# A feature pass by seven products per quadrant scheme, in two halves of tokens

## The reference, cut to what matters

```python
xn = _rms_norm(x, norm_g[l]) * (1.0 + sc_x) + sh_x
fx_in, fx_gate, qx, kx, vx, nx_gate = _split_proj(xn @ w_in[l])   # 1024 -> 6 x 512
qx = _rms_norm(_heads(qx), q_norm_g[l])                             # heads of 64
kx = _rms_norm(_heads(kx), k_norm_g[l])
f_out = _fourier(fx_in, w_four[l]) * jax.nn.silu(fx_gate)
na_out = _neighbourhood_attention(qx, kx, vx, ...) * jax.nn.silu(nx_gate)
```

## Time and profile before

| | us |
|---|---|
| median of three runs | 3400.0 (3398.42 to 3401.95) |
| profiled execution, device time | 3402.36 |
| its span, first to last instruction | 3400.6 |
| TensorE busy in it | 3111.9 (92%) |
| VectorE busy in it | 1514.0 (45%) |
| ScalarE busy | 941.8 (28%) |
| GpSimd busy | 795.5 (23%) |

### The profile page before, as it was taken

How to read it: one execution, slowest core, us unless ns; L and a number is a source line. 1 busy time by engine, 2 the same in 40 slices (tenths; PEclk the granted TensorE clock), 3 DMA queues, 4 the chain that set the end, 5 groups by cost and what they waited for, 6 DMA issues and landing times. The chain is left out here.

```text
span 3400.6 us, 39668 instructions
## 1 busy us (share of the span) xinstructions
PE 3111.9 (92%) x14503; PEld 2445.2 (72%) x14503; DVE 1514.0 (45%) x2504; ACT 941.8 (28%) x1520; POOL 795.5 (23%) x842
## 2 busy tenths in 40 slices
PE   3799999999988999775998999899999898999899
PEld 2588887888876666553897877677888675666687
DVE  6643333042306666386455222476000145777633
ACT  4422212110112334342222234322011133555400
POOL 5322222111112222265342222011111041000111
PEclk7899999999998999778898999999999998999999
DMA  7534335122243341314102666323211235776475
GB/s 272 184 97 116 102 101 180 61 77 75 75 127 87 90 105 55 90 47 97 43 26 82 200 185 208 109 112 123 74 74 74 99 102 134 155 158 142 112 199 148
DMA packets 325559, 390.82 MB, mean 115 GB/s; under 512 B 93879, under 2 KB 260264, under 8 KB 310696
## 3 DMA queue, kind: packets, MB, share of 16 engines
q1 hardware_dynamic: 320692, 387.11, 39.9%
q10 hardware_dynamic: 4704, 1.59, 0.2%
HBM read 256.77 MB, written 135.79 MB: 115 GB/s over the span
## 5 line engine op out<-in xcount | busy, mean ns | idle before, releaser
L691 PE MATMUL f_psum_out<-f_x_high,f_w_high 128*128 128x512 f32 (+1 forms) x1472 | 573.5, 390 | 18.8 <-DVE f_x_low L668 8.1
L691 PE MATMUL f_psum_out<-f_x_low,f_w_high 128*128 128x512 f32 (+1 forms) x1472 | 569.0, 387 | 0.0
L691 PE MATMUL f_psum_out<-f_x_high,f_w_low 128*128 128x512 f32 (+1 forms) x1472 | 568.6, 386 | 0.0
L691 PEld LDWEIGHTS f_psum_out<-f_x_high,f_w_high 128*128 128x128 f32 x1472 | 279.1, 190 | 77.9 <-issue 15.0
L691 PEld LDWEIGHTS f_psum_out<-f_x_low,f_w_high 128*128 128x128 f32 x1472 | 278.9, 189 | 56.5 <-issue 1.7
L691 PEld LDWEIGHTS f_psum_out<-f_x_high,f_w_low 128*128 128x128 f32 x1472 | 278.9, 189 | 55.5
L1351 PE MATMUL nbr_psum_o<-nbr_probT,nbr_v 128*128 128x512 f32 (+3 forms) x576 | 235.8, 490 | 0.0
L683 POOL CAST f_w_high<-f_w 128x1024 fp32r<-128x1024 f32 x41 | 42.6, 1040 | 747.8 <-PE f_psum_out L691 550.5
L532 PE MATMUL p_psum_proj<-p_w_high,p_h_high 128*128 128x512 f32 x512 | 207.5, 405 | 7.4 <-issue 4.0
L532 PE MATMUL p_psum_proj<-p_w_low,p_h_high 128*128 128x512 f32 x512 | 202.1, 395 | 0.0
L532 PE MATMUL p_psum_proj<-p_w_high,p_h_low 128*128 128x512 f32 x512 | 202.1, 395 | 0.0
(11 more groups left out here) (541 smaller groups left out, 6134.0 us busy)
## 6 DMA issues: line engine op xcount, KB each, us to landing
f_w<-in_w_fm SPq DMA_DIRECT2D x45, 512.0 KB, 5.7
side_ada_w<-in_w_ada_rows SPq DMA_DIRECT2D x24, 512.0 KB, 5.7
scratch_qkmT<-p_qkT_out SPq DMA_DIRECT2D x32, 384.0 KB, 4.6
scratch_z1T<-f_out SPq DMA_DIRECT2D x10, 1024.0 KB, 4.8
p_z<-scratch_z1T SPq DMA_DIRECT2D x16, 640.0 KB, 6.6
p_xt<-in_x SPq DMA_DIRECT2D x16, 512.0 KB, 3.9
p_staging<-in_w_tok SPq DMA_DIRECT2D x8, 1024.0 KB, 8.0
scratch_hT<-p_h_slot SPq DMA_DIRECT2D x16, 512.0 KB, 3.3
```

The source lines that it names most:

```text
L691: last = nc.tensor.matmul(self.p_out[b][:, n * BANK + lo:n * BANK + hi], self.w_parts[b][w_part][:, k, :], self.x_parts[x_part][:, n, k, l ...
```

## The change

The feature pass is made of 24 items: two halves of 1024 tokens by twelve pairs of blocks, in the order of `F2_ORDER`, so in each half first four pairs of queries and keys, then v, Fourier input and gates. An item's two blocks, the halves of its 1024 inputs, and pairs of neighbouring token tiles make two by two quadrants. The Strassen-Winograd scheme computes the four quadrants of the result from seven products of quadrants or of sums of quadrants. Each product is 4 x 3 matmuls of 128x512 into one of four PSUM banks (`product`); VectorE merges the banks into output rows in SBUF (`merge`: a copy for the first, one addition for each of the others and two for the sixth). The sums of weight quadrants are made by GpSimd for each item (`add_weights`), the seven high parts by ScalarE, the low parts by GpSimd. The sums of input quadrants (t1 to t4) are made once for each pair of tiles in the token pass by GpSimd (`combine`; the last pair by VectorE) and stored beside three quadrants as they are, so that seven arrays of 1 MB a half are loaded. The second half's arrays replace the first's during item 11.

An item's sums of squares have two matmuls for each row and lie at the start of the next item (row 1) and behind its first product (row 0). VectorE takes the reciprocals in pieces of 512 columns between the merges of the next item. Before the barrier four products of item 0 are done.

```diff
@@ -717,6 +717,117 @@
...
+class QuadrantPass:
+    A11, A12, A22, S1, S2, S3, S4 = range(7)
+    B11, B21, B22, T1, T2, T3, T4 = range(7)
+    PRODUCTS = ((A11, B11), (S2, T2), (A12, B21), (S3, T3), (A22, T4), (S1, T1), (S4, B22))
+    N, HK, BANKS = 7, KB // 2, 4
...
+    def load_x(self, sp, half, i):
+        if half:
+            sp.wait_ge(self.prod_ready, self.N * (half * self.per_half - 1) + i + 1)
+        sp.dma_start(self.x[i][0][:].rearrange("p t k c -> p (t k c)"),
+                     self.x_dram[self.PRODUCTS[i][1], :, half * 4 * BANK:(half + 1) * 4 * BANK]).then_inc(self.x_in[i], 16)
+
+    def round_x(self, act, half, i):
+        act.wait_ge(self.x_in[i], 16 * (half + 1))
+        self.nc.scalar.activation(self.x[i][1][:], self.x[i][0][:], ACT.Copy).then_inc(self.x_rounded, 1)
+
+    def rest_of_x(self, dve, half, i):
+        dve.wait_ge(self.x_rounded, self.N * half + i + 1)
+        self.nc.vector.tensor_tensor(self.x[i][2][:], self.x[i][0][:], self.x[i][1][:], ALU.subtract).then_inc(self.x_ready, 1)
...
+    def add_weights(self, pool, n):
+        nc, w = self.nc, self.w[n % 2]
+        a11, a12, a21, a22 = (w[:, m, k:k + self.HK] for m in range(2) for k in (0, self.HK))
+        s1, s2, s3, s4 = (self.sums[:, i] for i in range(4))
+        pool.wait_ge(self.w_in[n % 2], 16 * (n // 2 + 1))
+        pool.drain()
+        nc.gpsimd.tensor_tensor(s1, a21, a22, ALU.add)
+        nc.gpsimd.tensor_tensor(s3, a11, a21, ALU.subtract)
+        pool.drain()
+        nc.gpsimd.tensor_tensor(s2, s1, a11, ALU.subtract)
+        pool.drain()
+        nc.gpsimd.tensor_tensor(s4, a12, s2, ALU.subtract).then_inc(self.sums_ready, 1)
+
+    def round_w(self, act, n, i):
+        a = self.PRODUCTS[i][0]
+        if n:
+            act.wait_ge(self.prod_ready, self.N * (n - 1) + i + 1)
+        if a < self.S1:
+            act.wait_ge(self.w_in[n % 2], 16 * (n // 2 + 1))
+        else:
+            act.wait_ge(self.sums_ready, n + 1)
+        self.nc.scalar.activation(self.a_high[:, i], self.quadrant(n, a), ACT.Copy).then_inc(self.a_rounded, 1)
+
+    def rest_of_w(self, pool, n, i):
+        pool.wait_ge(self.a_rounded, self.N * n + i + 1)
+        self.nc.gpsimd.tensor_tensor(self.a_low[:, i], self.quadrant(n, self.PRODUCTS[i][0]), self.a_high[:, i], ALU.subtract)\
+            .then_inc(self.a_ready, 1)
+
...
+    def product(self, pe, n, i):
+        pe.wait_ge(self.a_ready, self.N * n + i + 1)
+        if n % self.per_half == 0:
+            pe.wait_ge(self.x_ready, self.N * (n // self.per_half) + i + 1)
+        if self.N * n + i >= self.BANKS:
+            pe.wait_ge(self.prod_free, self.N * n + i + 1 - self.BANKS)
+        a_parts, x_parts = (self.a_high, self.a_low), self.x[i][1:]
+        for k in range(self.HK):
+            for at, (w_part, x_part) in enumerate(PASSES):
+                last = self.nc.tensor.matmul(self.bank(n, i), a_parts[w_part][:, i, k, :], x_parts[x_part][:, :, k, :],
+                                             start=(k == 0 and at == 0), stop=(k == self.HK - 1 and at == len(PASSES) - 1))
+        last.then_inc(self.prod_ready, 1)
...
@@ tile_pass_2
+    def combine(eng, ops, j):
+
+        b11, b21, b12, b22 = (slot[b][:, k:k + HK] for b in range(2) for k in (0, HK))
+        t1, t2, t3, t4 = (combined[:, n] for n in range(4))
+        eng.wait_ge(combined_stored, 16 * (j + 1))
+        ops.tensor_tensor(t1, b12, b11, ALU.subtract)
+        ops.tensor_tensor(t3, b22, b12, ALU.subtract)
+        eng.drain()
+        ops.tensor_tensor(t2, b22, t1, ALU.subtract)
+        eng.drain()
+        ops.tensor_tensor(t4, t2, b21, ALU.subtract)
+        eng.drain().then_inc(combined_ready, 1)
...
+                else:
+                    sp.dma_start(quadrants[:, 2, of_pair], slot[1][:, HK:].rearrange("p k c -> p (k c)")).then_inc(slot_stored[1], 16)
+                    wait_apart(sp, combined_ready, j + 1, taken)
+                    sp.dma_start(quadrants[:, 3:7, of_pair], combined[:].rearrange("p s k c -> p s (k c)")).then_inc(combined_stored, 16)
...
+            def begin_next():
+                sp.wait_ge(w_ready, MB)
                 for b in range(2):
+                    sp.wait_ge(slot_stored[b], 16 * (NT // 4 + 1))
+                sp.wait_ge(combined_stored, 16 * (NT // 4 + 1))
+                fp.load_w(sp, 0)
+                fp.load_x(sp, 0, 0)
+
+            def go_on():
+                sp.wait_ge(gated[1], PAIRS)
+                fp.load_w(sp, 1)
+                sp.wait_ge(mix_ready[1], PAIRS)
+                sp.wait_ge(o_ready, NT - 1)
+                fp.load_x(sp, 0, 1)
                 sp.wait_ge(slices_used, 1)
+                fp.load_x(sp, 0, 2)
+                fp.load_x(sp, 0, 3)
 
             for k in range(BUFFERS, MB):
                 sp.wait_ge(w_ready, k - BUFFERS + 1)
                 begun.load_w(sp, k)
+            tiles(sp, tile, begin_next, go_on)
+            sp.wait_ge(slices_used, 2)
+            fp.load_x(sp, 0, 4)
+            fp.load_x(sp, 0, 5)
+            fp.load_x(sp, 0, 6)
...
+            for i in range(fp.BANKS):
+                fp.product(pe, 0, i)
+                if i == 0:
+                    turn_x(NT - 1)
...
+                fp.round_x(act, 0, 0)
+                for i in range(fp.N):
+                    fp.round_w(act, 0, i)
+                    if i == 1:
+                        fp.round_x(act, 0, 1)
+                fp.round_x(act, 0, 2)
+                fp.round_x(act, 0, 3)
...
+                if b == 0 and not first:
+                    wait_apart(pool, x_filled, 2 * j, taken)
+                    combine(pool, nc.gpsimd, j - 1)
...
@@ feature_pass_2
+F2_ORDER = (0, 1, 2, 3, 4, 5, 6, 7, 8, 9, 10, 11)
...
+            for n in range(LAST + 1):
+                aside(n - 1, 1)
+                for i in range(N):
+                    if n or i >= fp.BANKS:
+                        fp.product(pe, n, i)
+                    if i == 0:
+                        aside(n - 1, 0)
...
+            def after(n, b):
+                if kind(n) == "qk":
+                    act.wait_ge(out_ready[b], n + 1)
+                    if among(n, "qk"):
+                        act.wait_ge(low_ready[b], among(n, "qk"))
+                    nc.scalar.activation(work[b][:], out[n % 2][b][:], ACT.Square).then_inc(sq_ready[b], 1)
...
+            def empty(n, b):
+                if kind(n) == "qk":
+                    act.wait_ge(sum_ready[b], among(n, "qk") + 1)
+                    nc.scalar.activation(work[b][:], p_aux[b][:], ACT.Sqrt, scale=1.0 / HD, bias=g.eps[:]).then_inc(rms_ready[b], 1)
+                    act.drain().then_inc(aux_free[b], 1)
...
+            for n in range(LAST + 1):
+                empty(n - 1, 1)
+                for i in range(N):
+                    if n < LAST:
+                        fp.round_w(act, n + 1, i)
+                    if i == 0:
+                        empty(n - 1, 0)
+                    if n == fp.per_half - 1 and i:
+                        fp.round_x(act, 1, i - 1)
+                    if i == 5:
+                        after(n, 1)
+                if n == fp.per_half - 1:
+                    fp.round_x(act, 1, N - 1)
+                after(n, 0)
...
+                elif i == 5:
+                    dve.drain()
+                    nc.vector.tensor_tensor(column(second, 1), whole(u3), bank(n, 5), ALU.add)
+                    nc.vector.tensor_tensor(whole(u2), whole(u2), bank(n, 5), ALU.add).then_inc(fp.prod_free, 1)
+                    dve.drain().then_inc(out_ready[1], 1)
+                elif i == 6:
+                    nc.vector.tensor_tensor(column(first, 1), whole(u2), bank(n, 6), ALU.add).then_inc(fp.prod_free, 1)
+                    dve.drain().then_inc(out_ready[0], 1)
...
+            for n in range(LAST + 1):
+                refill = n == fp.per_half - 1
+                invert(n - 1, 1, 0)
+                for i in range(3):
+                    merge(n, i)
+                invert(n - 1, 1, BANK)
+                norm(n - 1, 1)
+                for i in range(3, N):
+                    merge(n, i)
+                    if i == 3:
+                        invert(n - 1, 0, 0)
+                    if i == 4:
+                        invert(n - 1, 0, BANK)
+                    if i == 5:
+                        norm(n - 1, 0)
+                    if refill:
+                        fp.rest_of_x(dve, 1, i - 3)
+                if refill:
+                    for i in range(N - 3, N):
+                        fp.rest_of_x(dve, 1, i)
...
```

More of the change, by code:

```diff
@@ L2364, in _ @@
+            sp.wait_ge(high_stored, 32 * among(LAST + 1, "qk"))
+            for n in range(2):
+                for b in range(2):
+                    sp.wait_ge(stored[n][b], 16 * (LAST + 1) // 2)
         @block.tensor
         def _(pe):
[L2366 to L2373 removed]
@@ L2375, in turn_v @@
-            def turn_v(j, b):
-                pe.wait_ge(vT_ready[b], j - FIRST_V + 1)
-                for n in range(NT):
```

(6 more changed lines are left out.)

371 lines of the change are left out of this document (213 added, 158 removed).

## The result

The changed kernel took 3478.7 us (3475.1 to 3484.1, four runs) where the kernel before took 3401.0 in the same job: a ratio of 1.023 (95% interval 1.0212 to 1.0248, written in square brackets below), slower by 78 us. The forecast was 3455, in a range from 3385 to 3485: the time lies in it, 6 us under its upper end.

A forecast was written before the change was run, and what follows sets the result against it. The feature pass was taken as bound by its count of products. Terms -54.4 + 3.3 + 69 + 39 - 6 + 5 - 0.5 = +55 on a median of 3400.0 gave 3455 us, range 3385 to 3485.

The forecast's parts named there:

- Products: Feature pass: 2016 full products instead of 2304, 240 fewer behind the barrier at 0.2267 us each, -54.4 us.
- the rival of slow products: Feature pass: moving operand in four runs of 128 columns slows products 5%, 23 us more, 3478 us; chance 0.05.
- Rounds: Eight queries' and keys' items: VectorE sets the pace, 32 us a round against TensorE's 22.9, +69 us (+33 to +89).
- the rivals in which it doesn't: Queries' and keys' items: VectorE's round stays under TensorE's, so the saved products come through, 3386 us; chance 0.13.
- in which only its 26.6 us of work count: Queries' and keys' items: VectorE's pieces overlap without stalls, 3419 us; chance 0.15.
- sum without a slow start, 30.8: Queries' and keys' round: VectorE's work 26.6 us plus stalls of 2.4 and 1.8 us.
- The two stalls: Queries' and keys' round: VectorE idles 2.4 us for ScalarE's square root and 1.8 us for TensorE's third product.
- busy shares: Queries' and keys' items: VectorE busy over 80% and TensorE under 80%, as a sign of the forecast.
- Slow start of TensorE: Queries' and keys' rounds: low clock after idling delays the third product 1.7 us each round; without it 13 us lower.
- Token pass: SyncE waits for GpSimd's sums before the next loads, delaying y, 6.5 us six times, +39 us (+30 to +50).
- Handover: Last tile to work behind the barrier: about L + 49 instead of L + 54.8, -6 us (-12 to +3).
- refill: Between the halves: 7 MB of new input and VectorE's rests delay the first merge of item 12, +5 us (+2 to +12).

The follow-up runs named there:

- the halved reciprocals: Changed kernel with the second 512 columns of each row's reciprocal replaced by a multiply and add to a constant: 3443.4 us.
- The late store: Changed kernel with the store of the four input sums, and its wait for GpSimd, moved behind the next tile's loads in SyncE's queue: 3428.1 us.
- GpSimd small: Changed kernel with GpSimd's sums and low parts of the weights cut to 8 of each 128 columns from item 1 on: 3466.5 us.
- the first reordering: Changed kernel with mixed item order, row 1 normalised one item later, the late store, and pieces and weights rounded behind the last tile's work at handover: 3399.8 us.
- the third order: Changed kernel, VectorE reordered, with the late store; at handover pieces 1, 2 rounded before the last fill, weights, piece 3 behind: 3407.3 us; with the last order 3361.8.
- the last order: Changed kernel with mixed item order and normalising spread, row 1's reciprocals early behind the item's last merge: 3415.0 us; with the late store and the third order, 3361.8.

## Why the prediction was right

**Products.** Right: 19.0 us for each item of 84 products, so the rival of slow products is out. Its 3478 lies close to the result, but by chance of the sum.

**Rounds**, +69 forecast, +83.0 measured: six rounds of 33.0 to 34.4 us where 32 was taken, two of 31.4 where it was 30. The mechanism is the one named. That VectorE sets the pace in the tail is shown by the halved reciprocals (-45.3 us); the rivals in which it doesn't, or in which only its 26.6 us of work count, are out. The prediction's own sum without a slow start, 30.8, is what the two rounds without one show: 32.0, less 1.3 for GpSimd.

That 1.3 is the term that the prediction lacked. The trace before had none of GpSimd's work at that place, and I took VectorE's durations as they stood; beside GpSimd the subtraction of row 1 takes 2.14 us and its scaling 1.78. Taking GpSimd's work out shortened the tails by 10.2 us in sum, most of the 14 that were missing. The Trainium skill's "SBUF — State Buffer", section "Who interferes with whom", says that a VectorE instruction with two inputs in SBUF contends with a GpSimd instruction that reads SBUF; the trace agrees: the sixth merge (L2675), with one input in PSUM, takes 686 to 689 ns in all 24. That rule stood open to the prediction.

The two stalls were counted as VectorE's own, 2.4 us behind ScalarE and 1.8 behind TensorE, and added. In the round the first lies ahead of the second: without it, VectorE waits as much longer for TensorE. Undoing it gave nothing. The sum was right all the same, since only the moment at which the third product is ready counts: 13.6 us after the end of the sixth merge by the prediction, 14.9 from its start, and 15.1 measured. Its busy shares missed: VectorE over 80% and TensorE under 80% were forecast, and they are 75 and 79% against 80 and 76%.

**Slow start of TensorE.** It was counted at 1.7 us a round by the clock of the earlier trace rows, of which the taken 32 keeps 1.2. The rule of "TensorE: Matmul & The Clock Gate" in the Trainium skill, section "HAM oscillation", that it is paid in each round, agrees with the trace: behind each of the six waits of 8.67 us the sums took 3.48 to 3.75 us instead of 1.88. It is not paid in the first round of each half, which follows no such wait. In the six it costs 1.0 to 2.4 us, 1.85 in the mean, because the sums and the first three products lie in the head, where VectorE waits for TensorE. That is 11.1 us in sum and close to the 13 of the prediction. This is worked out from the rounds with and without it; keeping TensorE busy removed it in two rounds alone, and no run removed it in all.

**Token pass**, +39 forecast, +43.5 measured, by the mechanism named: SyncE waited 5.7 us for GpSimd's sums ahead of y. The late store takes it all back. In the turn shown y is issued 6.4 us behind the store of x2T instead of 0.73, so 5.7 later (5.1 forecast), and it lands 5.85 us after that instead of 4.39: over the six turns it lands 1.4 us later in the mean, with the bytes ahead of it (1 forecast). The two were not tried apart.

**Handover**, -6 forecast, -0.6 measured, and **refill**, +5 forecast, +9.1 measured (21.2 + 25.9 against 2 x 19.04). In both the steps were placed by single transfers and the rounding behind them. With GpSimd small the second refill step is 20.1 instead of 25.9, so most of it hangs on GpSimd, which the prediction had declared hidden. By the traces it is GpSimd's slowing of VectorE: the seven rests (L780) take 20.6 us instead of 16.2, and TensorE's wait of 7.06 us there ends with VectorE's first merge behind them, not with weights. For the handover the trace shows where the forecast steps slipped, with L, the start of the last tile, at 2139.58: the last tile's square at L + 30.1 (27 forecast), ScalarE's last rounding at L + 46.0 (42), and from VectorE's last rest, which ends at 2190.17, to TensorE's first product 3.6 us (1.7). In the last of these stands a wait that the prediction had at nothing: all four banks are full at the barrier, so TensorE needs the first merge, and VectorE has a load of the gains ahead of it.

```profile
2192.67 0.15 DVE L2683 TENSOR_SCALAR f_gain<-f_gain 128x1 f32<-128x1 f32 x1 [2.50 <-DMA f_gain<-in_qk_gain]
2192.91 0.69 DVE L2660 COPY f_out<-f_psum_prod 128x512 f32<-128x512 f32 x1
```

Moving that load was not tried. From the residual sum ahead of the last tile's products to the first sixth merge it is 62.8 us in the changed kernel and in the first reordering, 59.6 with the late store alone, and 57.4 and 58.3 in the two kernels with the third order. Other kernels with an unchanged handover have up to 65.2, so part of this is scatter.

The net error of +27 on the forecast's +55 is the sum of those sizes (14 + 4.5 + 5.4 + 4, less small ones). All four errors have the same sign, so hardly anything cancelled; the forecast was right on the mechanism and low on each size.

## What to carry to other kernels

When a change gives an engine work beside another's products, cost its order and not its sum: here the same instructions on VectorE made two items with and without normalisation cost 53, 50, 48 or 43 us together. In the last order long operations stand where the engine waited for products before, and no block of 12 us holds up the merges; that this is why it wins is read from the traces, in which TensorE's waits of 3.1 and 5.8 us in these pairs are down to 1.9 at most. A wait that is placed before loads in SyncE's queue costs its full length each turn; put stores whose data is late behind the loads of the next turn. When an idle engine is found, ask what would be late if that wait were gone before counting it: VectorE's wait for ScalarE's root could be removed for nothing, while TensorE's slow start cost its full length, although VectorE had more work than TensorE in the round. And judge an experiment by whether it did what it was meant to: the products that should keep TensorE's clock up did so in two rounds of six, and those two show the price.

## What the runs showed of the hardware

A reciprocal of 128x512 in fp32 took 3.34 to 3.35 us in all 32 instances of the changed kernel, five times an add of the same size (0.69); 2048 columns took 12.95. The fp32 subtraction 128x1024 from SBUF went from 1.22 to 2.11 us with GpSimd's subtraction beside it, which took 1.57 to 1.62 us there instead of 1.29; beside VectorE's subtractions of 128x2048 at the refill it took up to 3.34. Which of the two pays depends on who begins. The cast of 128x1024, with one input, took 0.69 us in all 16 instances of the changed kernel and 1.60 to 1.68 in all 16 of the kernel with early reciprocals (alone, without the late store). VectorE and GpSimd in order of time, first in the changed kernel, then in that one:

```profile
2269.68 0.69 DVE L2635 CAST f_high<-f_out 128x1024 fp32r<-128x1024 f32 x1
2269.87 1.62 POOL L813 TENSOR_TENSOR f_a_low<-f_sums,f_a_high 128x512 fp32r<-128x512 f32 x1 [9.80 <-ACT f_a_high L809]
```
```profile
2313.47 1.92 POOL L813 TENSOR_TENSOR f_a_low<-f_sums,f_a_high 128x512 fp32r<-128x512 f32 x1 [1.43 <-ACT f_a_high L809]
2314.31 1.63 DVE L2639 CAST f_high<-f_out 128x1024 fp32r<-128x1024 f32 x1
```

The cast that begins 0.19 us ahead keeps its 0.69, and GpSimd takes 1.62 instead of 1.29; the cast that begins 0.84 us behind GpSimd's operation takes 0.94 longer. What that costs the second kernel was not measured; its pairs take at most 2 us more than the 42 that TensorE needs.

After 3.11 us of waiting for a merge, the row of 2295.87 above, TensorE's products began every 0.43 us instead of 0.2267 for 5 us, at a granted clock of 0.50. Waits of about that length were followed by a slow start in some rounds and not in others. Behind 28 products without a gap and then 2.23 us of waiting, the sums were slow in four rounds of six (a granted clock of 0.64 over the 3 us at 2243.70, 1.00 at 2276.77). With the halved reciprocals TensorE waits 3.20 us at that place, and five of six were followed by the lower clock.
